# A two-block transformer kernel: every large SBUF tensor begins on a multiple of 1024 bytes

## What is computed

```python
# first block
proj = rms_norm(x, g) @ w_in                      # 1024 x 3080
att  = causal attention, 8 heads of 64            # on q, k with partial rotary
hm   = mLSTM, 4 heads, q.k of 64, v of 128, gated
x    = x + rms_norm(concat(att, hm) @ w_out)      # 1024 x 1024
x    = x + rms_norm(relu(rms_norm(x) @ w_up)**2 @ w_down)   # 1024 x 4096 x 1024
# second block, two layers
mod  = silu(c) @ ada_w[l] + ada_b[l]              # 1024 x 6144, shifts, scales, gates
z    = (rms_norm(x) * (1 + scale1) + shift1) @ w_in[l]       # 1024 x 4608
y    = sigmoid gates of (differential attention @ w_attn_o) and
       (causal convolution of 31 taps, layer norm, silu) @ w_conv_o
x    = x + (1 + gate1) * (y @ w_out[l])
x    = x + (1 + gate2) * ((silu(f_gate) * f_up) @ w_ffn_out[l])   # width 2816
```

## The kernel before, in words

| tensor | begins at byte | past a multiple of 1024 | past a multiple of 64 |
|---|---|---|---|
| raw, hi, lo (24576 bytes each) | 16512, 41088, 65664 | 128 | 0 |
| cst (4132 bytes) | 108672 | 128 | 0 |
| x, act_hi, act_lo, hf, sq, rstd, tabs | 112832, 121024, 129216, ... | 192 | 0 |
| qk1, qk2, v1, v2, gates, mqk, mv, mo | 159136, ... | 416 | 32 |
| att_hi, att_lo, hng | 184864, 188960, 184864 | 544 | 32 |
| cacc, csq, on, sB, pB | 192384, ... | 896 | 0 |
| u_hi, u_lo (32768 bytes each) | 159136, 191904 | 416 | 32 |

## Time and profile before

### The profile page before, as it was taken

One profiled execution on the slowest core, in us unless ns is written; L12 is line 12 of the kernel. 1 busy time (PEld: TensorE's weight loads), 2 busy tenths in 40 slices (PEclk: granted clock), 3 DMA queues, 4 the chain that ended last, 5 costly groups with the idle time before them and its releaser, 6 DMA issues.

```text
span 1080.6 us, 19232 instructions
## 1 busy us (share of the span) xinstructions
PE 1058.0 (98%) x8174; PEld 1007.3 (93%) x8174; DVE 833.6 (77%) x1117; ACT 525.7 (49%) x625; POOL 29.8 (3%) x54
## 2 busy tenths in 40 slices
PE   7999999999999999999999999999999999999998
PEld 6878899999998989989999999999898899999998
DVE  5878699988775899968898887869999576555552
ACT  5554665554424544554644433464456455444441
POOL 5100000000000010000000000000000000000000
PEclk9999999999999999999999999999999999999998
DMA  8566348889893464428599998846442375666551
GB/s 278 166 215 235 117 176 298 281 288 307 292 353 116 161 200 130 145 88 303 182 368 311 331 335 295 271 135 230 161 156 79 118 254 184 197 190 193 173 175 39
DMA packets 137473, 230.37 MB, mean 213 GB/s; under 512 B 7107, under 2 KB 60715, under 8 KB 137389
## 3 DMA queue, kind: packets, MB, share of 16 engines
q1 hardware_dynamic: 135060, 227.05, 62.1%
q0 software_dynamic: 1408, 0.79, 0.4%
q10 hardware_dynamic: 921, 1.32, 0.4%
HBM read 227.29 MB, written 1.06 MB: 211 GB/s over the span
## 4 chain that ended last, share of the span: by engine, by line
PE 71%; DVE 18%; ACT 7%; DMA 2%; issue 1%; SPq 1%; DVEq 0%; POOL 0%; ACTq 0%
PE mm L435 66%; DVE lo L1296 7%; DVE cacc L1386 5%; ACT hi L840 3%; PE mm L478 1%; DMA raw<-in_w_in_dram 1%; DMA raw<-in_w_out_dram 1%; ACT pB L919 1%; DVE sB L1394 1%; DVE qk L1413 1%; DVE hf L1411 1%; DVE qk L1412 1%; DMA swap<-qk 1%; PE pv L576 1%; PE pa L542 0%
## 5 line engine op out<-in xcount | busy, mean ns | idle before, releaser
L435 PE MATMUL mm<-act_hi,hi 128*128 128x256 f32 x1760 | 489.1, 282 | 5.8 <-ACT act_hi L908 2.3
L435 PE MATMUL mm<-act_hi,lo 128*128 128x256 f32 x1760 | 484.2, 279 | 0.0
L435 PE MATMUL mm<-act_lo,hi 128*128 128x256 f32 x1760 | 467.5, 279 | 0.0
L1296 DVE TENSOR_TENSOR lo<-raw,hi 128x2048 fp32r<-128x2048 f32 (+1 forms) x159 | 359.6, 2265 | 133.0 <-ACT hi L840 130.3
L840 ACT ACTIVATE hi<-raw 128x2048 fp32r<-128x2048 f32 (+1 forms) x159 | 300.2, 1891 | 247.3 <-PE mm L435 194.4
L435 PEld LDWEIGHTS mm<-act_hi,hi 128*128 128x128 f32 x1760 | 331.4, 188 | 11.5 <-issue 7.1
L435 PEld LDWEIGHTS mm<-act_hi,lo 128*128 128x128 f32 x1760 | 331.9, 189 | 0.3
L435 PEld LDWEIGHTS mm<-act_lo,hi 128*128 128x128 f32 x1760 | 321.0, 188 | 0.0
L435 PE MATMUL mm<-u_hi,hi 128*128 128x256 f32 x608 | 171.9, 283 | 0.0
L435 PE MATMUL mm<-u_hi,lo 128*128 128x256 f32 x608 | 171.4, 282 | 0.0
L435 PE MATMUL mm<-u_lo,hi 128*128 128x256 f32 x608 | 171.4, 282 | 0.0
(11 more groups left out here) (280 smaller groups left out, 908.6 us busy)
## 6 DMA issues: line engine op xcount, KB each, us to landing
ada_raw<-in_ada_w_dram SPq DMA_DIRECT2D x128, 384.0 KB, 5.4
raw<-in_w_ffn_in_dram SPq DMA_DIRECT2D x88, 512.0 KB, 5.2
raw<-in_w_in_dram SPq DMA_DIRECT2D x39, 1024.0 KB, 5.3
raw<-in_w_ffn_out_dram SPq DMA_DIRECT2D x20, 1024.0 KB, 5.9
raw<-in_w_up_dram SPq DMA_DIRECT2D x16, 1024.0 KB, 6.4
raw<-in_w_down_dram SPq DMA_DIRECT2D x16, 1024.0 KB, 7.5
raw<-in_w_out_dram SPq DMA_DIRECT2D x12, 1024.0 KB, 5.8
raw<-in_w_in_dram SPq DMA_DIRECT2D x16, 512.0 KB, 5.9
```

Of the source, the lines that this page charges most:

```text
L435: ins = pe.matmul(o, w[:, kk, fs], a[:, k, :], start=(k == 0 and i == 0 and f % 2 == 0), stop=(ends and i == len(pairs) - 1), skip_group_c ...
L1296: v(dve.tensor_tensor(lo[:, c % RING, 0:nk, :], raw[:, c % RING, 0:nk, :], hi[:, c % RING, 0:nk, :].bitcast(F32), ALU.subtract), "lo_done")
```

## The change

The small tensors and `cst` are allocated ahead of `raw`, followed by a pad of 608 bytes that nobody uses. In `mixA`, `wg`, `gbias` and `acol` go from the middle to the end. No instruction, wait or DMA is added or taken away.

```diff
@@ -235,19 +235,7 @@
         pa = ps("pa", [P, GF])
         pv = [ps(f"pv{i}", [P, GF]) for i in range(3)]
 
-        raw = sb("raw", [P, RING, CK, GF])
-        hi = sb("hi", [P, RING, CK, GF], F32R)
-        lo = sb("lo", [P, RING, CK, GF], F32R)
-        ada_raw = sb("ada_raw", [P, ADA_RING, ADA_W])
-        ada_acc = sb("ada_acc", [P, LAYERS, ADA_W])
         cst = sb("cst", [P, C_ALL])
-        x = sb("x", [P, KD, S])
-        act_hi = sb("act_hi", [P, KD, S], F32R)
-        act_lo = sb("act_lo", [P, KD, S], F32R)
-        hf = sb("hf", [P, 4, S])
-        sq = sb("sq", [P, KD, S])
-        rstd = sb("rstd", [P, 2, S])
-        tabs = sb("tabs", [P, 2, 2 * S])
         parT = sb("parT", [P, NROW])
         adabT = sb("adabT", [P, NMOD + ADA_P])
         modT = sb("modT", [P, NMOD])
@@ -258,6 +246,19 @@
         nlam = sb("nlam", [P, LAYERS])
         gain0 = sb("gain0", [P, KD])
         token_root = sb("token_root", [P, TT])
+        sb("line_pad", [P, 152])
+        raw = sb("raw", [P, RING, CK, GF])
+        hi = sb("hi", [P, RING, CK, GF], F32R)
+        lo = sb("lo", [P, RING, CK, GF], F32R)
+        ada_raw = sb("ada_raw", [P, ADA_RING, ADA_W])
+        ada_acc = sb("ada_acc", [P, LAYERS, ADA_W])
+        x = sb("x", [P, KD, S])
+        act_hi = sb("act_hi", [P, KD, S], F32R)
+        act_lo = sb("act_lo", [P, KD, S], F32R)
+        hf = sb("hf", [P, 4, S])
+        sq = sb("sq", [P, KD, S])
+        rstd = sb("rstd", [P, 2, S])
+        tabs = sb("tabs", [P, 2, 2 * S])
 
 
         mixA = ExitStack()
@@ -272,15 +273,12 @@
         mqk = sb("mqk", [P, 4, S], on=mixA)
         mv = sb("mv", [P, TT, GF], on=mixA)
         mo = sb("mo", [P, 4, S], on=mixA)
-        wg = sb("wg", [P, KD, F0 + MH], on=mixA)
         att = ExitStack()
         att_hi = sb("att_hi", [P, 4, S], F32R, on=att)
         att_lo = sb("att_lo", [P, 4, S], F32R, on=att)
         att.close()
         hng = sb("hng", [P, KD, S], on=mixA)
-        gbias = sb("gbias", [MH, 2], on=mixA)
         gate = sb("gate", [4, 8, S], on=mixA)
-        acol = sb("acol", [P, TT, 4], on=mixA)
         start = ExitStack()
         rows = sb("rows", [P, P], on=start)
         adab = sb("adab", [P, P], on=start)
@@ -300,6 +298,9 @@
         pM = sb("pM", [P, 2, 3 * P], on=mixA)
         emA = sb("emA", [P, 2, S], on=mixA)
         lams = sb("lams", [1, 16], on=mixA)
+        acol = sb("acol", [P, TT, 4], on=mixA)
+        gbias = sb("gbias", [MH, 2], on=mixA)
+        wg = sb("wg", [P, KD, F0 + MH], on=mixA)
         hmA = qk1[:, 0:2, :]
         mixA.close()
         mixB = ExitStack()
```

## The result

The changed kernel takes 1097.0 us (median of 4 runs, 1096.4 to 1098.3) against 1079.05 (1072.9 to 1085.6): a ratio of 1.0186, with a 95% interval of 1.0134 to 1.0237. It is slower, and its runs lie closer together. Ratios and intervals here go by the runs in the faster of two states alone, medians and ranges by all runs, so that a ratio can differ from the quotient of the medians (here 1.0166). The rival with its sign is "the two streams collide", which had 1104 us; the forecast had 1056.

What follows compares the result with a forecast made beforehand. TensorE was taken to bound the kernel. Faster single-pass matmuls gave 12.3 + 1.7 + 8.8 + 0.4 + 1.6 = 24.8 us, so 1080.6 - 24.8 = 1056 us; the range was 1023 to 1084.

Steps and rivals of the forecast that it cites:

- the two streams collide: Moving tile and weights begin at equal places, so every matmul goes to 0.1201 us: 22.4 us and 0.9 slower, 1104; chance 0.20.
- What bounds: Whole kernel: TensorE, busy 1058.0 of 1080.6 us, sets the time; layout counts only through the cost of one matmul.
- the first term: Single-pass matmuls on act, u, att and the weights, moved to multiples of 1024, run at 0.1133 us: 24.8 us less.
- the 12.3 us for act: 2798 long-pace matmuls on act, outside the attention units, each get 4.4 ns faster: 12.3 us less.
- the 8.8 for the rest of u: 1296 matmuls on u outside layer 1's down product each get 6.8 ns faster: 8.8 us less.
- the 1.6 us for the 512-column products: 192 products of 512 columns, taken at 0.228 us, each get 3.7%, 8.5 ns, faster: 1.6 us less.
- csq, on and the others lose their alignment: nothing: Small tensors that TensorE reads in two passes go to 32 off a multiple of 64: 0.1 us, taken as nothing.
- VectorE and ScalarE do not see the start byte: VectorE and ScalarE operands move, but their operations keep their durations: nothing.
- What is late next: At 0.1133, VectorE (97% in the up stage) and DMA (345 GB/s in layer 0's ffn) still fit; otherwise 3.4 us each return.
- No effect: Rival: u's slower pace comes from something else its stages share, so the time stays 1080.6 us; chance 0.06.
- The extra could go altogether (0.108): Rival: alignment brings single-pass matmuls to 0.108 us, VectorE then stops the up stage at 0.110: 1023 us; chance 0.10.
- The time around the span: Difference between the profiled span of 1080.6 us and the runs' median of 1080.7, taken as 0.1 us.

Runs made afterwards that it cites:

- the sweep: Separate kernel without the two blocks: TensorE streams 40 matmuls per stretch, moving and weight tiles at varied start places; a finer one used 16-byte steps. No kernel time.
- the 112-byte kernel: Changed kernel with act, att and u placed 112 bytes past the weights modulo 256: 1061.6 us, 0.9816 of the kernel before.
- the kernel with 64 bytes: Changed kernel with 64 bytes more between ada_acc and x, so act, att and u begin 64 past the weights: 1080.0 us, 0.9952 of the kernel before.
- 64 and 192 bytes: Changed kernel with 64 or 192 bytes more between ada_acc and x, moving act, att and u off the weights: 1080.0 us and 1069.6 us.

## Why the prediction was wrong

- *What bounds.* Right. TensorE's pace set the time, up and down: 1.5% more busy time, 1.3% more span.
- *The failing step* is the first term: "Between these ends I take 0.1133, act's short pace". I read u against act as "less aligned costs more" and carried the line on to 1024. The two rows also fit a difference from the weights, 288 and 64 bytes, and the prediction said so itself under its last rival. u's place is 32 modulo 256 off the weights, and act's is 64; the sweep puts 32 at 116.7 and 64 at 117.8, so they are two points of a curve that goes up and down several times in 256 bytes, with no slope to carry on; and part of u's distance from act was what act's pace hands on. Equal places, which no row of before showed, measured 0.1200 at the upper bound of the range that I had set for the pace. Of the terms, the 12.3 us for act and the 1.7 for layer 1's u came with the other sign (2.3 and 3.4 ns more for each matmul), so did the 0.4 for att, and the 8.8 for the rest of u came to nothing; act that had the short pace, put at nothing, lost 1810 x 6.7 ns = 12 us. Only the 1.6 us for the 512-column products had the right sign, at about 1.1, and by luck: they gained because their best place is another one.
- *The collision rival* had place and pace: 0.1201 against 0.1200 measured, and its point of decision, act above 0.1177, was met. That the two read streams collide fits and is not shown. Its 1104 us are 7 too many. It let the attention units lose time that VectorE covers (672 x 2.4 ns = 1.6 us), left out that nothing of theirs came in the first 164 us, and had the 512-column products 0.9 us longer where they became about 1 shorter. What stood against it, that u is farthest from equal, rested on a period of 512; modulo 256 u is the nearer, with 32 against 64. It had 0.20, and with that it deserved more.
- *The first 164 us.* The sum takes 480 x 4.4 ns = 2.1 us and att's 0.4 from them. The up stage begins at 163.6 us after and at 164.2 before, though each matmul on act ahead of it took some 2 to 6 ns more. The granted clock hides what the places did there: before, 10 x 0.13 + 20 x 0.09 = 3.1 us of full speed are missing (an estimate), after, none. All of TensorE from 20 to 30 and from 60 to 80 us, first before, then after:

```profile
20.00:30.00 10.00, 10.00 (x78) 0.87 0.72 240
60.00:80.00 20.00, 18.53 (x115) 0.91 0.57 184
20.00:30.00 10.00, 10.00 (x84) 1.00 0.72 234
60.00:80.00 20.00, 18.62 (x123) 1.00 0.56 184
```

- *csq, on and the others lose their alignment: nothing.* Right: the two-pass records on csq start every 0.216 us, as before, though their difference from `raw` went from 0 to 224 modulo 256.
- *VectorE and ScalarE do not see the start byte.* Right for VectorE: 2264 ns against 2265, 478 against 479. ScalarE's busy time is 525.5 us against 525.7.
- *What is late next.* Right in both, as the 112-byte kernel showed: VectorE at 97% of the up stage and the DMA at 344 GB/s held the pace of 0.1133.
- *No effect.* Wrong for float32r: places that all lie on multiples of 16 bytes differ by 5.9%. The 0 was my reading of the page and not what it says: of the start rule the Trainium skill's page "SBUF — State Buffer", section "Operand start alignment", writes "This is about legality, not speed". The same page of the Trainium skill, section "Who interferes with whom", calls TensorE's two read ports, for the moving operand and for the weights, independent. The Trainium skill's page "TensorE: Matmul & The Clock Gate", section "Step-by-step: what each phase is for", says that loading the next weights "doesn't steal SBUF read bandwidth from the running matmul". The sweeps show an interaction that neither names: the same moving tile of 256 columns has another pace when only the weights' place changes (120.0 ns for 64 against 64, 117.8 for 64 against 0). What in it waits for what is not seen.
- *The extra could go altogether (0.108).* Not at any place tried; 0.1133 is the lowest. The 109.2 ns that stood beside it are, in the Trainium skill's page "TensorE: Matmul & The Clock Gate", section "Back-to-back issue gap", the gap of a single matmul, and the section says that in a stream the weight loads set the spacing too. No run here came to it.
- *The time around the span.* I took it as 0.1 us. The runs after have it at 2.1 (1097.0 and 1094.9), so by the same 2.1 (an estimate) the profiled execution of before stood near 1083, inside its own spread. The dips of the granted clock above are part of what it had over the median. That is 2 us of the sum, without weight here.

The paces account for the difference between the two spans but for 1 us. 2798 x 2.3 + 1810 x 6.7 + 528 x 3.4 ns - 1.2 us = 19.1 us is the sum over the whole kernel, and 14.3 came. The starts of the streams in the two timelines say where the rest went. Ahead of the up stage lie 480 x 2.3 + 96 x 6.7 ns - 0.6 us (half of the 512-column products) = 1.1 us of the sum, and 0.6 us went the other way. The attention units hold another 96 x 6.7 ns = 0.6 us; the eight of a layer, up to the next long stream, took 90.3 and 88.9 us before (from 405.3 and 774.0) and 89.1 and 88.7 after (from 408.1 and 778.9), 1.4 us less. 19.1 - 1.1 - 0.6 - 0.6 - 1.4 = 15.4. Why the attention units became shorter was not looked into.

Had the pace been the forecast's 0.1133 throughout, the time would still not have been 1056: the 112-byte kernel has that pace and takes 1061.6 us.

## What to carry over

Where single-pass float32r matmuls of 256 columns set the time, the place that counts is the moving tile's against the weights', modulo 256 bytes; round numbers for both put them at the worst one measured, 0.1200. Measure the pace start to start, over all stretches, because one layout can have two paces, and take a place that has the short one every time. Two rows that differ in two things are not a slope: before carrying a trend on, name what else the rows have in common, and look for a row at the point where the change lands.

## What the runs showed of the hardware

- 256-column float32r matmuls with 128x128 weights start every 113.3 to 120.0 ns at a granted clock of 1.00. Which it is depends on the difference of places modulo 256 bytes: 120.0 at 0 and 96, 113.3 at 112 every time, 113.3 or 117.8 at 192 and at 64.
- Where a place has two paces, a stream as a rule keeps the one it begins with: 1577 matmuls at 0.1177 in one case. One stream of the kernel with 64 bytes went from 0.1133 to 0.1178 on its way. Where a stream passes to another place without a pause, the pace that it had counts: u, 32 off, had 120.0 ns after act's 117.8 and 116.7 after its 113.3. The kernels with two paces have runs that differ by 16 us (before, 1072.9 to 1089.5 over all of its runs; 64 and 192 bytes likewise), those with one pace at each place differ by 2. That the draw of paces is the cause fits, but only the profiled run's paces are seen. The dips of the granted clock, 3.1 us of full speed before and 1.8 with 112 bytes, are too small for it. Why a stream starts in one or the other was not found.
- 512 columns: 226.7 ns at a difference of 0, 233.3 at 192. The best place for 256 columns is not the best for 512.
- Two-pass float32 matmuls showed none of this: 0.216 us for 256 columns at differences of 0 and of 224 bytes.
